# Laying out the S5 mixer's inputs before 1/rms is known, and shifting tokens by DMA

## The reference, cut to what matters

```python
# between layer 1's MLP and the S5 mixer
x = x + sqrelu_mlp(rmsnorm(x, norm_mlp[0]), mlp_w1[0], mlp_w2[0])
h = rmsnorm(x, norm_mix[1])            # x * rsqrt(mean(x*x) + eps) * g
u = h.reshape(B, S, S5_GROUPS, 16)     # the mixer's inputs, 16 channels a group
...
# in the hybrid layer: u is h @ w_in, the RWKV columns are shifted by one token
def _token_shift(u, mu):
    prev = jnp.pad(u, ((0, 0), (1, 0), (0, 0)))[:, :-1]
    return u + (prev - u) * mu
```

## Time and profile before

| | |
|---|---|
| three runs | 3373.81, 3379.45, 3381.02 us; median 3379.45 |
| profiled execution | 3374.61 us, of which 3372.9 us are its span |
| TensorE busy | 94% of the span |
| VectorE, ScalarE, GpSimd busy | 56%, 41%, 9% |
| mean granted TensorE clock | 0.954 of full |
| DMA | 574 MB, 170 GB/s in the mean |
| chain of work that ended last | TensorE 86%, GpSimd 5%, VectorE 4% |

### The profile page before, as it was taken

One profiled execution on the slowest core, in us unless ns is written; L12 is line 12 of the kernel. 1 busy time (PEld: TensorE's weight loads), 2 busy tenths in 40 slices (PEclk: granted clock), 3 DMA queues, 4 the chain that ended last, 5 costly groups with the idle time before them and its releaser, 6 DMA issues.

```text
span 3372.9 us, 42502 instructions
## 1 busy us (share of the span) xinstructions
PE 3167.5 (94%) x16187; PEld 2637.6 (78%) x16187; DVE 1904.5 (56%) x2148; ACT 1376.4 (41%) x1834; POOL 313.8 (9%) x328
## 2 busy tenths in 40 slices
PE   8999999999999668999999999999999996869898
PEld 7887877888888567888888888878877785858786
DVE  5555669656665565555555555654455455575464
ACT  5555443444434333444343434444434553020134
POOL 2000006100019753000000000000000000000000
PEclk9999999999999867999999999999999998988799
DMA  7554576756667733566666666566655553010164
GB/s 236 175 169 146 178 197 215 237 180 193 209 217 202 243 111 119 190 210 185 194 187 193 187 190 188 187 192 189 187 170 167 160 180 123 14 41 1 62 237 150
DMA packets 310966, 574.49 MB, mean 170 GB/s; under 512 B 31552, under 2 KB 50240, under 8 KB 309248
## 3 DMA queue, kind: packets, MB, share of 16 engines
q1 hardware_dynamic: 287232, 524.95, 49.4%
q0 software_dynamic: 4976, 23.86, 2.4%
q10 hardware_dynamic: 18576, 23.12, 2.2%
HBM read 549.30 MB, written 20.45 MB: 169 GB/s over the span
## 4 chain that ended last, share of the span: by engine, by line
PE 86%; POOL 5%; DVE 4%; issue 2%; ACT 2%; DMA 1%; ACTq 1%; SPq 0%; DVEq 0%; POOLq 0%
PE acc L882 23%; PE acc L883 23%; PE acc L889 23%; PE tp L897 2%; PE acc L1410 1%; PE tp L1419 1%; POOL tmade L821 1%; PE acc L1418 1%; PE acc L1499 1%; PE acc L1500 1%; PE acc L1506 1%; POOL tmul L819 1%; PE wk L1162 1%; DVE wL L2160 1%; DVE A L2909 1%
## 5 line engine op out<-in xcount | busy, mean ns | idle before, releaser
L2160 DVE TENSOR_TENSOR wL<-raw,wH 128x1024 fp32r<-128x1024 f32 (+1 forms) x968 | 1223.0, 1271 | 1191.4 <-ACT wH L1534 1182.2
L1534 ACT CAST wH<-raw 128x1024 fp32r<-128x1024 f32 (+1 forms) x968 | 1008.9, 1045 | 1454.6 <-PE acc L889 1295.2
L882 PE MATMUL acc<-wH,xH 128*128 128x512 f32 (+1 forms) x2208 | 872.6, 396 | 13.4 <-ACT wH L1534 8.6
L883 PE MATMUL acc<-wH,xL 128*128 128x512 f32 (+1 forms) x2208 | 859.3, 390 | 0.0
L882 PE MATMUL acc<-wH,hH 128*128 128x512 f32 x1536 | 603.2, 393 | 6.5 <-DVE hL L2214 6.5
L883 PE MATMUL acc<-wH,hL 128*128 128x512 f32 x1536 | 600.3, 391 | 0.0
L889 PE MATMUL acc<-wL,xH 128*128 128x512 f32 (+1 forms) x2208 | 589.1, 389 | 4.3 <-DVE wL L2160 4.3
L882 PEld LDWEIGHTS acc<-wH,xH 128*128 128x128 f32 x2208 | 417.4, 189 | 104.4 <-issue 13.4
L889 PEld LDWEIGHTS acc<-wL,xH 128*128 128x128 f32 x2208 | 414.4, 189 | 90.9 <-DVE wL L2160 4.7
L883 PEld LDWEIGHTS acc<-wH,xL 128*128 128x128 f32 x2208 | 417.7, 189 | 84.9 <-issue 1.9
L889 PE MATMUL acc<-wL,hH 128*128 128x512 f32 x1536 | 412.1, 390 | 0.0
(11 more groups left out here) (446 smaller groups left out, 2636.8 us busy)
## 6 DMA issues: line engine op xcount, KB each, us to landing
raw<-in_mlp_w_dram SPq DMA_DIRECT2D x512, 512.0 KB, 3.8
raw<-in_w_in_dram SPq DMA_DIRECT2D x192, 512.0 KB, 3.5
raw<-in_a_w_in_dram SPq DMA_DIRECT2D x96, 512.0 KB, 3.7
raw<-in_b_w_glu_dram SPq DMA_DIRECT2D x64, 512.0 KB, 3.6
raw<-in_a_w_out_dram SPq DMA_DIRECT2D x32, 512.0 KB, 3.8
raw<-in_w_out_dram SPq DMA_DIRECT2D x32, 512.0 KB, 4.0
raw<-in_w_proj_fox_dram SPq DMA_DIRECT2D x16, 512.0 KB, 4.5
raw<-in_w_proj_rwkv_dram SPq DMA_DIRECT2D x16, 512.0 KB, 4.1
```

Source lines behind the costliest of these rows:

```text
L882: nc.tensor.matmul(bank, aH[:, k, rows], wH[:, j % SPLIT, u, 0:n], start=k == 0, stop=False)
L883: nc.tensor.matmul(bank, aL[:, k, rows], wH[:, j % SPLIT, u, 0:n], start=False, stop=False)
L1534: nc.scalar.copy(wH[:, j % SPLIT, :, 0:n], raw[:, j % RAW, :, 0:n]).then_inc(high_done, 1)
L2160: nc.vector.tensor_tensor(wL[:, j % SPLIT, :, 0:n], raw[:, j % RAW, :, 0:n], wH[:, j % SPLIT, :, 0:n].bitcast(F32), ALU.subtract).then_inc ...
```

## The change

Four things are changed.

1. *The seam.* `norm` and `added` are not called there any more. From chunk 29 on, VectorE writes quarter q of xn as X * gain, without 1/rms, right behind the chunk that follows or makes that quarter (`lead_gain`); ScalarE squares quarters 0 to 2 there too, and loads the root's table. GpSimd instead of SyncE issues the 32 copies into U2, quarter by quarter. 1/rms is brought into U2's order of tokens by VectorE (`rs_by`), two matmuls with a 0/1 matrix `choose` and a copy into four columns, `rs4`; ScalarE's copy into `up` becomes four activations for each block, each with a scale column.
2. *GpSimd's tables.* The rotation powers are made before the bT transfers and written differently (54 small operations, several merged), stored to a DRAM scratch, since `bpad` takes their place, and read back ahead of the Toeplitz copies. The load of the gains is issued there too. VectorE waits for the rotation tables in chunk 29 instead of at the seam.
3. *The token shift.* TensorE's products with `shift` and `corner` for chunks 8 to 15 are gone. GpSimd issues two transfers for each chunk, from `stg` to `prev`: rows 0 to 126 of both halves to rows 1 to 127, and row 127 of the first half to row 0 of the second. VectorE subtracts, multiplies by mu and adds, over both halves at once.
4. ScalarE's stream in the first MLP calls its function after every chunk of all four blocks, where it did so in the first block alone.

```diff
+S5_TURNED = 18 + 54
+S5_CLEAR = S5_TURNED + 1
+S5_CHOSEN = S5_CLEAR + 7
...
@@ SyncE, s5_stream
-                for i, q in enumerate((0, 2, 1, 3)):
-                    sp.wait_ge(xn_done, MT * QT * 2 + MT * (i + 1))
-                    h, cols = q // 2, slice((q % 2) * NW, (q % 2 + 1) * NW)
-                    for m in range(MT):
-                        rows = slice(64 * h + 32 * m, 64 * h + 32 * m + 32)
-                        for e in range(S5_L):
-                            sp.dma_start(U2[rows, e, cols], xn[e:P:S5_L, m, q * NW:(q + 1) * NW]).then_inc(u_in[q], 16)
@@ GpSimd, s5_tables
+                def squared():
+                    nonlocal e0, flip
+                    new = epow[:, flip]
+                    flip = 1 - flip
+                    ta, tb = ptmp[:, 0, 0:2 * S5_PAIRS].rearrange("p (c n) -> p c n", c=2), ptmp[:, 1, 0:S5_PAIRS]
+                    link(nc.gpsimd.tensor_tensor(ta, e0, e0, ALU.mult))
+                    link(nc.gpsimd.tensor_tensor(tb, e0[:, 0], e0[:, 1], ALU.mult))
+                    link(nc.gpsimd.tensor_tensor(new[:, 0], ta[:, 0], ta[:, 1], ALU.subtract))
+                    link(nc.gpsimd.tensor_tensor(new[:, 1], tb, tb, ALU.add))
+                    e0 = new
+
+                pool.wait_ge(s5_back, 2)
+                squared()
+                squared()
                 pool.wait_ge(s5_out, 80)
+                link(nc.gpsimd.memset(powr[:, :, 0, :, 0:1], 1.0))
+                link(nc.gpsimd.memset(powr[:, :, 1, :, 0:1], 0.0))
+                for a in range(2):
+                    for lvl in range(3):
...
+                        link(nc.gpsimd.tensor_tensor(ta, old, by[0], ALU.mult))
+                        link(nc.gpsimd.tensor_tensor(tb, old, by[1], ALU.mult))
+                        link(nc.gpsimd.tensor_tensor(new[:, 0], ta[:, 0], tb[:, 1], ALU.subtract))
+                        link(nc.gpsimd.tensor_tensor(new[:, 1], tb[:, 0], ta[:, 1], ALU.add))
+                        if a == 0 or lvl < 2:
+                            squared()
+                    if a == 0:
+                        pool.wait_ge(s5_back, 18)
+                        for r in range(2):
+                            for twice in range(2):
+                                pool.dma_start(bT[:, r, :, twice], bb_dram.rearrange("(k e) c r s -> r (e c) k s", e=8)[r]).then_inc(s5_bin, 16)
+                pool.dma_start(p_dram, powr[:]).then_inc(powr_out, 16)
+                pool.wait_ge(powr_out, 16)
                 link(nc.gpsimd.memset(bpad[:], 0.0))
+                link(nc.gpsimd.memset(choose[:], 0.0))
...
                 pool.wait_ge(powers_out, 32)
                 pool.wait_ge(kernels_out, 32)
+                pool.dma_start(powr[:], p_dram).then_inc(powr_in, 16)
+                pool.dma_start(gain[:], norms[2].broadcast_to([P, D])).then_inc(gain_in, 16)
                 nc.gpsimd.memset(Tt[:], 0.0).then_inc(toep_clear, 1)
...
+                pool.wait_ge(powr_in, 16)
...
+                for b in range(2):
+                    pool.wait_ge(phases_out[b], 16 * 4)
+                for q in range(QT):
+                    h, cols = q // 2, slice((q % 2) * NW, (q % 2 + 1) * NW)
+                    for m in range(MT):
+                        pool.wait_ge(xn_done, MT * (QT * 2 + q) + m + 1)
+                        rows = slice(64 * h + 32 * m, 64 * h + 32 * m + 32)
+                        for e in range(S5_L):
+                            pool.dma_start(U2[rows, e, cols], xn[e:P:S5_L, m, q * NW:(q + 1) * NW]).then_inc(u_in[q], 16)
@@ GpSimd, new
+            def previous_tokens():
+                for n in range(8):
+                    par = n % 2
+                    pool.wait_ge(acc_free, 2 * (SECOND_FILL + 8 + n) + 6)
+                    pool.wait_ge(shift_out, 2 * n + 1)
+                    pool.dma_start(prev[1:P], stg[0:P - 1, par]).then_inc(prev_in, 16)
+                    pool.dma_start(prev[0:1, 1], stg[P - 1:P, par, 0]).then_inc(prev_in, 16)
@@ TensorE, ahead of the mixer
+            pe.wait_ge(s5_pool, S5_CHOSEN)
+            pe.wait_ge(group_free, n0 + 2)
+            pe.wait_ge(rs_made, 1)
+            for m in range(MT):
+                last = nc.tensor.matmul(tp[0][:, 0, 0:S5_L], choose[:, m], rs_by[:, m], start=m == 0, stop=m == MT - 1)
+            last.then_inc(rs_summed, 1)
@@ TensorE, chunks 9 to 16 of w_in
-                if 9 <= c <= 16:
-                    return shifted(c - 1)
@@ ScalarE
+                if c >= 29:
+                    s5_square(c - 29, t.fill + 28)
+                if c == 31:
+                    nc.scalar.activation(small[:, 104 + t.norm:105 + t.norm], eps, ACT.Sqrt)
...
-            norm(added)
+            s5_square(3, t.fill - 4)
+            act.wait_ge(ssum_done, t.norm + 1)
+            nc.scalar.activation(std, ss, ACT.Sqrt, bias=eps, scale=1.0 / D).then_inc(std_done, 1)
+            t.norm += 1
+            act.wait_ge(rs_summed, 1)
+            nc.scalar.copy(rs4, tp[0][:, 0, 0:S5_L]).then_inc(rs_in, 1)
+            act.wait_ge(rs_in, 1)
...
-                SACT.mark(s_act, nc.scalar.copy(up[:, b % 2].rearrange("p (a s c) -> p a s c", a=4, s=S5_L),
-                                                U2[:, :, b * 64:(b + 1) * 64].rearrange("p s (a c) -> p a s c", a=4)), "p", b)
+                for e in range(S5_L):
+                    last = nc.scalar.activation(dst[:, :, e], U2[:, e, b * 64:(b + 1) * 64].rearrange("p (a c) -> p a c", a=4),
+                                                ACT.Copy, scale=rs4[:, e:e + 1])
+                SACT.mark(s_act, last, "p", b)
@@ VectorE
+                if c == 29:
+                    for b in range(2):
+                        dve.wait_ge(phases_out[b], 16 * 4)
+                    dve.wait_ge(gain_in, 32)
+                    lead_gain(0, fill=t.fill + 28)
+                if 29 <= c:
+                    lead_gain(c - 28, fill=t.fill + c)
...
-                dve.wait_ge(shift_done, n + 1)
...
+                dve.wait_ge(prev_in, 32 * (n + 1))
+                if n == 0:
+                    dve.wait_ge(shift_out, 1)
+                o = dst[:, :, (n % 2) * NW:(n % 2 + 1) * NW]
+                mu = mixmu[:, n * NW:(n + 1) * NW].unsqueeze(1).broadcast_to([P, MT, NW])
+                nc.vector.tensor_tensor(o, prev[:], stg[:, c % 2], ALU.subtract).then_inc(shift_mul, 1)
+                dve.wait_ge(shift_mul, 2 * n + 1)
+                nc.vector.tensor_tensor(o, o, mu, ALU.mult).then_inc(shift_mul, 1)
+                dve.wait_ge(shift_mul, 2 * n + 2)
+                nc.vector.tensor_tensor(o, o, stg[:, c % 2], ALU.add).then_inc(shift_out, 2)
```

More of the change, by code:

```diff
@@ L311, in build @@
         powr = at("mix", 0, "powr", [P, 2, 2, S5_PAIRS, 8])
-        ptmp = at("mix", 8, "ptmp", [P, 2, S5_PAIRS, 4])
-        epow = at("mix", 10, "epow", [P, 4, S5_PAIRS])
+        p_dram = nc.dram_tensor("p_scratch", (P, 2, 2, S5_PAIRS, 8), F32, kind="Internal").ap()
+        ptmp = at("mix", 8, "ptmp", [P, 2, 2 * S5_PAIRS * 4])
+        epow = at("mix", 12, "epow", [P, 2, 2, S5_PAIRS])
         tmul = at("mix", 12, "tmul", [P, 2, 8, S5_N])
@@ L328, in build @@
         m01 = at("low", 0, "m01", [P, S5_N])
+        choose = at("low", 0.5, "choose", [P, MT, P])
         U2 = at("mix", 16, "U2", [P, S5_L, D // 2])
@@ L748, in s5_tables @@
                 pool.dma_start(g_dram[:, 0], gA[:]).then_inc(s5_out, 16)
[L750 to L753, removed]
-                pool.wait_ge(s5_out, 80)
-                link(nc.gpsimd.memset(bpad[:], 0.0))
+                e0 = srs[:, 1:3]
+                flip = 0
+                def squared():
[8 more added lines that the diff above has]
+                    e0 = new
@@ new lines, in s5_tables @@
+                assert n[0] == S5_TURNED, n[0]
+                pool.dma_start(p_dram, powr[:]).then_inc(powr_out, 16)
+                pool.wait_ge(powr_out, 16)
+                link(nc.gpsimd.memset(bpad[:], 0.0))
+                link(nc.gpsimd.memset(choose[:], 0.0))
+                for m in range(MT):
+                    part = choose[:, m].rearrange("p (h a i) -> p h a i", h=2, a=MT)[:, :, m]
+                    link(nc.gpsimd.memset(part, 1.0))
+                    for base, step in ((0, -S5_L), (S5_L - 1, S5_L)):
+                        link(nc.gpsimd.affine_select(out=part, in_=part, compare_op=ALU.is_ge, fill=0.0, base=base,
+                                                     pattern=[[0, 2], [step, 32]], channel_multiplier=-1 if step > 0 else 1))
@@ L1225, in stg_turn @@
                 return mid
-            def shifted(c):
-                def mid():
-                    pe.wait_ge(acc_free, 2 * (f0 + c) + 6)
-                    if c > 8:
-                        pe.wait_ge(shift_out, 2 * (c - 8))
-                    for m in range(MT):
-                        bank = wk[m][:].rearrange("p a s -> p (a s)")
-                        last = nc.tensor.matmul(bank, shift[:], stg[:, c % 2, m], start=True, stop=m == 0)
-                        if m:
```

(8 more changed lines are left out.)

95 lines of the change are left out of this document (45 added, 50 removed).

## The result

The changed kernel took 3329.7 us in the median of four runs (3315.01 to 3344.17), beside 3376.63 for four runs of the kernel before on the same chip: ratio 0.9862, 95% interval 0.9831 to 0.9893. The forecast was 3334, its range 3322 to 3350. The four runs are not spread around their median, though: 3315.01, 3315.72, 3343.68, 3344.17. The profiled execution is the one of 3343.68, span 3341.9, granted clock 0.953. It is 31.0 shorter than the profiled execution before, where the sum of the forecast said 44.

What follows compares the result with a forecast made beforehand. TensorE, 94% busy, was taken to bound the kernel. 24.1 + 20.9 - 1 = 44 us off the profiled 3374.6 gives 3330.6, or 3335 from the median of three; forecast 3334, range 3322 to 3350.

Steps and rivals of the forecast that it cites:

- the sum of the forecast: Whole kernel: 24.1 + 20.9 - 1 = 44 us off the profiled execution, 3374.6 to 3330.6.
- The seam: Between first MLP and S5 mixer: TensorE's first transpose at 1162.3 instead of 1186.76, gain 24.1 us.
- The mixer's loop: S5 mixer's 16 blocks: 10.4 us more on ScalarE, hidden in its idle time before the gelus, cost nothing.
- Rival (a): Half-late: U2's last quarter (6 us), copies that don't fit (10.4) or 3 us scales; 3340 to 3355, chance 0.17.
- The token shift: Eight chunks each lose six matmul passes on TensorE, 2.61 us a chunk, 20.9 us in all.
- The tail of 1 us: Chunk 16's shifted row holds back chunk 17's first split: 1 us off the gain, between 0 and 2.6.
- Rival (b): Shifted rows' 127-partition transfers go through one DMA engine: 32.8 us a chunk against 24.3, kernel 3423; chance 0.08.
- Powers and phases: GpSimd's rotation powers move before bT; tables end near 1101, landed by 1106, cost nothing.
- the 8 claimed: Margin in us at chunk 29: tables landed by 1106, VectorE waits for them after its addition ending at 1114.2.
- Rival (c): Tables miss chunk 29 if GpSimd's work runs 15 us longer, each us onto TensorE once; 3337 to 3360, chance 0.05.
- part 2: Powers and phases: tables start behind the Toeplitz copies, at 1016.0 plus 1.2 us for two more issues.
- The 4.8 us: Median of three before, 3379.45, lies 4.8 above the profiled execution; by that basis 3335 instead of 3330.6.

Runs made afterwards that it cites:

- b3: Changed kernel with all 32 U2 transfers issued only after the last quarter's products; 3352.5 us, ratio 0.9912.
- c3: Changed kernel a third time, nothing altered; 3340.59 us.
- a1: Changed kernel measured again, nothing altered; 3337.59 us.
- a2: Changed kernel with the old token shift put back; 3359.58 us, ratio 0.9951.
- a3: Kernel before with the new token shift alone; 3356.46 us, ratio 0.9932.
- c2: Changed kernel with two more GpSimd products, results overwritten, in each of the eight rotation-table blocks; 3338.92 us.
- b1: Changed kernel with the gain load behind the rotation tables and the eight Toeplitz copies issued one behind each table block; 3328.66 us.
- c4: b1 measured again, nothing altered, beside c3 on the same chip; 3330.39 us.
- a4: Changed kernel with the 1 MB gain load issued behind the rotation tables' loop; 3334.54 us.
- b4: Changed kernel with the shifted rows' two transfers issued by ScalarE instead of GpSimd, the first over 127 partitions; 3463.21 us, ratio 1.028.
- c1: b4 with the first transfer of each pair cut into 112 and 15 partitions; 3345.68 us.

## Why the prediction was right, point by point

**The seam** held: 24.4 measured where 24.1 was worked out. The chain of small operations is as listed; the scales were ready 3.7 us after the last addition's end (1165.68 to 1169.34), in the forecast 3.5 (1157.55 to 1161.1). U2's last quarter went out in 4.17 us instead of 6.1 (0.52 an issue, not 0.76), its last piece landed after 7.3, at 1177.53, and the third rotation, at 1181.4, did not wait for it. b3 shows that the quarters carry 17 of it.

**The mixer's loop** held: from its start to the GLU's first addition it is 0.85 shorter, in c3 0.25 shorter and in a1 0.2 longer, so the four scaled copies cost nothing. Rival (a) has no part in the time.

**The token shift** held: low-half matmuls 2.72 apart, 21.7 us a chunk. The first full unit behind `lo` (the short chunk's result) is 19.1 us earlier against the second MLP's end than before (-16.6 to -35.7), 20.5 in a1, 19.1 in c3, 20.9 expected. What is missing goes with a half-clock stretch at the start of this matrix: 6.8 us in the changed kernel's first profile and in c3, 3.4 in a1 and in the kernel before, and half of the difference is 1.7. a2, without the new shift, has the 6.8, too, and loses 1.3 there. The tail of 1 us didn't come: the eighth chunk gave its 2.6 like the others, against a3's expectation of seven. Rival (b) was false on GpSimd's queue and true on ScalarE's. There the stage is 107 us longer than before (-13.6 to 93.3), where 68 had been worked out: a chunk takes 37.6 us instead of 32.8, because the raw loads and ScalarE are held up as well. The reason given against this rival was too wide: not every transfer of GpSimd shows a rate of many engines, since 64 KB in 13.5 us is 4.9 GB/s, below the 18.4 worked out for one.

**Powers and phases** held, and the wait in chunk 29 was empty: the last table landed at 1107.6, and VectorE asked at 1122.1. Of these 14.5 us of margin 8 are the pile-up's, which held VectorE up, so without it 6.4 are left of the 8 claimed. That also flatters c2, where 21 us later cost nothing. Rival (c) has its mechanism, too, and its threshold: a wait of 5.0 us in chunk 29 is covered by the splits in hand (b1, c2), one of 7.6 puts 2.3 onto TensorE (c4), which fits with each us beyond 5 once, though one run shows it. The powers took 49.6 us (596.0 to 645.6), and `bpad` was clear at 656.7, 26 ahead of VectorE's first write.

**The step that failed** is in part 2: "1016.0 plus 1.2 for two more issues". The two loads were priced by their issues alone, 1.2 us, and not by what 2 MB more on the DMA engines do to the raw tiles beside them. The price was 8.1 us in the first profile (6.1 of TensorE's wait and 1.6 for the clock), 7.4 to 9.6 in the three. The rows for it were at hand: Toeplitz copies of up to 13.5 us landing beside raw tiles that TensorE needs every 2.7 us. With it the sum is 24.4 + 20.9 - 8.1 = 37.2; the three profiles have 37.5, 36.4, 37.6 at the heads' begin.

**The rest is the heads' clock.** The 6.5 us from -37.5 to -30.9 come from there: the changed kernel's first profile spends 164 us at half clock among the heads, the kernel before 147. The distance to 3315 comes from there, too, by a4's profile; the changed kernel's own executions near 3315 have no profile, only their mean clock, 0.961 to 0.963 where the profiled one has 0.953. The median of four lies at 3329.7 because it is the mean of 3315.72 and 3343.68, one of each group, so its nearness to 3334 is luck. Over all 13 executions of the unaltered changed kernel the median is 3338.69. That is 8.1 above the sum's 3330.6, about what the pile-up cost; the agreement to a tenth is chance. The range holds both. The 4.8 us that I allowed for the median of three runs before were not needed: the medians of 9 to 11 runs before are 3374.15 to 3374.71, at the profiled execution's 3374.61.

## What to carry to other kernels

A transfer that is moved has two prices, its issue on the queue and its share of the DMA engines at the new place. Look at what the engines carry there already, and at how much slack the loads that TensorE lives on have; here spreading eight copies over 82 us gave back what sending them together, next to 2 MB more, had cost. Before a difference of executions is explained by the change, compare starts of the same instruction along the span: here it showed 37 us that are the change's and up to 28 that aren't. And a transfer of 127 partitions is better cut in 112 and 15 if it goes by ScalarE's queue: in b4, without the cut, the heads begin 129 us later than in c1.

## What the runs showed of the hardware

- 508 KB from 127 partitions to 127: 6.1 us to landing from GpSimd, 30 to 34 us from ScalarE until VectorE could use them, and 4.5 us from ScalarE as 112 rows, with 5.1 for the 15. From ScalarE the 127 packets ran one at a time. In the slow case the queue's next issue, 2 KB, was held for 8.9 to 13.2 us.
- One and the same code among small matmuls can lose a stretch of 37.5 us at half clock or not, 15 to 17 us of time in the first row block (from the second to the third group in the table), from one execution to the next.
- Eight copies of GpSimd's issued within 6 us, behind 2 MB issued just before, held 512 KB loads of SyncE's back to 16.7 to 22.9 us and TensorE for 4.8 to 6.8. One copy every 12 us beside the same 2 MB left TensorE without a gap.
